# An expert tile built from the first two token tiles, a sixth weight buffer, and stores moved within the queue

## The chip, the core and the metric

The kernel runs on one core of a Trainium2 chip. The metric is the time of one execution on the device in microseconds (us); smaller is better. Engines are TensorE (PE in the rows, with PEld for its weight loads), VectorE (DVE), ScalarE (ACT), GpSimd (POOL) and SyncE (SP). A "q" behind an engine is its queue of DMA issues.

## The reference

One layer of an encoder over 512 tokens of width 1024, all float32: RMSNorm, one input projection, latent attention (8 heads, dense) and 2-D neighbourhood attention (8 heads), output projection added to x, and a mixture of experts:

```
p_g = softmax(h @ w_rg + b_rg)            # 4 groups, the best one is taken
le  = logits of the 4 experts of that group; top 2, softmax weights
a, u = h @ w_gate[e], h @ w_up[e]         # 1024 -> 256, for the token's 2 experts
x = x + sum over them of weight * (silu(a) * u) @ w_down[e]
```

There are 16 experts. Each has 2.1 MB of gate and up weights and 1.05 MB of down weights.

## The kernel before

Tokens are handled in T = 4 tiles of 128. After attention of a token tile, its sum x + attention (in `x_sb`) is normed, a router product gives logits, VectorE picks groups and experts (`logits_out`), TensorE computes each row's rank within its expert by products with a triangle of ones (`ranks`), VectorE turns ranks into row numbers (`ranks_out`), and GpSimd sends the tile's rows, with their weights and token numbers, to these places of a DRAM buffer `slot_rows` (`dispatch`, two sends a token tile, one for each of a token's two experts). That buffer was zeroed at the start.

Each expert has CAP = 96 places. They are read back as ITEMS = 12 expert tiles of 128 rows; tile g holds blocks of 32 rows (BLK), block b belonging to expert (4g + b) // 3. What overflows an expert goes to further tiles: number 12 always runs, up to EXTRA - 1 more run only when needed (`passes`). So tile 0 needs rows of all four token tiles.

For each expert tile g: its rows are loaded (`load_x`, on ScalarE's queue, all behind `s_disp`, the landing of all eight sends), TensorE turns them (`x_turns`), VectorE copies them out with the gain (`x_read`), `gate_up` multiplies (8 steps, 4 blocks), ScalarE does `silu`, VectorE the product (`hidden`), TensorE turns it (`hid_turns`), VectorE copies it (`hidden_read`), `down` multiplies, ScalarE and VectorE scale the two halves with the row's weight (`left_y`, `right_y`), and GpSimd adds the rows to the output in DRAM (`add`). TensorE's order is written out: gate_up(g), down(g-1), x_turns(g+2), hid_turns(g).

Expert weights pass through RING = 5 buffers each, filled in SP's queue, in order: buffer n % RING is asked for again when the last tile using its old expert is through gate_up (`s_gu`) or down (`s_dn`). Experts 0 to 4 are loaded during attention. SP's order at the end of attention is: load_gu(3), load_dn(3) and (4), load_gu(2), load_dn(2), load_gu(4), then the four stores of the sums to the output.

Every engine works through its own list in order; a wait holds all that is behind it.

Of the kernel before, what the change touches and what calls it, by code (L numbers as in the profile page):

```python
# [6 lines left out]
P = 128  # L7
# [39 lines left out]
EXTRA = TOP * SEQ // (CAP + 1)  # L47
FAR = 1 << 20
RING = 5
# [6 lines left out]
NK = K_MINE + ITEMS  # L56
# [7 lines left out]
def build(nc, x, x_turned, cols_d, rows_d, rope_d, rpb_d, consts_d, w_in_lat, w_in_k, w_in_q, w_in_v, w_qb, w_kvb, w_out, w_r,  # L64
# [8 lines left out]
    with ctx:  # L73
# [55 lines left out]
        junk = at(151, D_MODEL)  # L129
# [7 lines left out]
        sil = [at(140, F), at(141, F)]  # L137
        hid = [at(142, F), at(143, F)]
        hidT = [at(144, 2, P), at(145, 2, P)]
        y_sb = [at(110, D_MODEL), at(114, D_MODEL), at(136, D_MODEL)]  # L140
# [3 lines left out]
        x_hit = at(152, EXTRA, E)  # L144
        tag_sb = at(153, TILES, 2)
        tag_row = at(153.25, TILES, 1).bitcast(i32)
        x_prod = at(151, T, TOP, E)
# [35 lines left out]
        counts = sm(E)  # L183
        nmax = sm(2, H)
# [14 lines left out]
        GU = [bank[2], bank[3]]  # L199
# [35 lines left out]
        s_disp, s_over = sem("rows_dispatched"), sem("overflow_dispatched")  # L235
# [6 lines left out]
        s_add = [sem(f"y{r}_added_to_out") for r in range(3)]  # L242
# [20 lines left out]
        order += [("ms", 1, T - 1), ("h2", T - 1, 0), ("h2", T - 1, 1)]  # L263
        turn = {key: n for n, key in enumerate(order)}
        BY_ACT = ("k", "q", "nak", "naq")
# [44 lines left out]

        def turn_x(g, b):
            return 2 * g + b if g < 2 else 3 * g - 2 + b if g <= LAST else 3 * g + b

        def turn_h(g):
            return 3 * g + 6 if g < LAST - 1 else 2 * LAST + g + 2 if g <= LAST else 3 * g + 2

        def loads_of(g):

            return [(4 * g + b) // 3 if g < ITEMS else E + g - ITEMS for b in range(4)]

        def last_item(n):
            return (CAP * n + CAP - 1) // P if n < E else ITEMS + n - E

        def added_before(g):

            return 16 * (g // 3)
# [29 lines left out]
        def _(sp):  # L356
# [64 lines left out]

            sp.wait_ge(s_y, group["a", T - 1, 1] + 1)
            load_gu(3, 3)

# [15 lines left out]
            for g in range(LAST):  # L440
                for n in range(RING, E + 1):
# [3 lines left out]
                for n in range(RING, E + 1):  # L445
                    if last_item(n - RING) == g - 1:
                        sp.wait_ge(s_dn, 2 * g)
                        load_dn(n, expert(n))
# [13 lines left out]
            for g in range(LAST - 2, LAST + 1):  # L462
                sp.wait_ge(s_add[g % 3], added_before(g) + 16)

        @block.gpsimd
        def _(pool):
# [105 lines left out]
            def dispatch(t):  # L572
                pool.wait_ge(s_zero, 16)
                pool.wait_ge(s_h2s, t + 1)
                pool.wait_ge(s_wts, t + 1)
                pool.wait_ge(s_slot, t + 1)
                for k in range(TOP):
                    send(t, k, slots[0], ITEMS, s_disp)
# [23 lines left out]
            def add(g):  # L602
# [5 lines left out]
                    in_=y_sb[g % 3], in_offset=None,  # L608
                    bounds_check=SEQ - 1, oob_is_err=False, compute_op=ALU.add).then_inc(s_add[g % 3], 16)

            def added(g):

                pool.wait_ge(s_add[g % 3], added_before(g) + 16)
# [22 lines left out]
        def _(act):  # L636
# [77 lines left out]
            def x1_squares(t):  # L714
                act.wait_ge(s_x1, group["b", t, 1] + 1)
                link(nc.scalar.activation(junk, x_sb[:, t, :], ACT.Square, scale=D_MODEL ** -0.5,
# [101 lines left out]
            h2_rows(T - 1)  # L818
            top_exps(T - 1)
            nc.scalar.activation(junk[:, 0:1], junk[:, 0:1], ACT.Silu)  # L820

            def load_x(g):
                if g >= 3:
                    act.wait_ge(s_tt, turn_x(g - 3, 1) + 1)
# [3 lines left out]
            act.wait_ge(s_disp, 16 * TOP * T)  # L828
            for g in range(3):
                load_x(g)  # L830
            load_x(3)
# [7 lines left out]
            def left_y(g):  # L839
                act.wait_ge(s_dn, 2 * g + 1)  # L840
                act.wait_ge(s_tag, g + 1)
                if g >= 3:
                    act.wait_ge(s_add[g % 3], added_before(g))
                nc.scalar.activation(y_sb[g % 3][:, 0:512], YR[g % 2][0][:, :], ACT.Copy,
                                     scale=tag_sb[:, g, 0:1]).then_inc(s_ya, 1)

            for g in range(LAST + 1):
                if g == LAST:
                    left_y(g - 1)
                silu(g)  # L850
                if g + 4 <= LAST:
# [14 lines left out]
        def _(dve):  # L866
# [298 lines left out]
            def extras_out():  # L1165

                dve.wait_ge(s_counted, 1)
                nc.vector.tensor_copy(counts, bank[3][:, 0:E]).then_inc(s_countr, 1)
# [59 lines left out]
            def right_y(g):  # L1228
                dve.wait_ge(s_dn, 2 * g + 2)
                if g >= 3:  # L1230
                    dve.wait_ge(s_add[g % 3], added_before(g))
                nc.vector.tensor_scalar(y_sb[g % 3][:, 512:1024], YR[g % 2][1][:, :], tag_sb[:, g, 0:1], None,  # L1232
# [14 lines left out]
            x_read(0)  # L1247
            tile_tags(0)
            x_read(1)
            tile_tags(1)  # L1250
            extras_out()
            for g in range(LAST + 1):
# [3 lines left out]
                if 0 < g < LAST:  # L1256
# [5 lines left out]
                if g == 0:  # L1262
                    slots_out()
# [11 lines left out]
        def _(pe):  # L1275
# [150 lines left out]
            def side_turn(key):  # L1426
# [19 lines left out]
                if kind == "h2":  # L1446
                    pe.wait_ge(s_x1, group["b", t, b] + 1)
                    transposes(key, four(x_sb[:, t, :], b))

# [46 lines left out]
            def ranks(t):  # L1496
# [3 lines left out]
                for i in range(t + 1):  # L1500
                    last = nc.tensor.matmul(KB_OF[t][:, 32:32 + E], konst[:, K_ONE:K_ONE + P] if i < t else konst[:, K_TRI:K_TRI + P],
                                            sels[:, i, 0:E], start=(i == 0), stop=(i == t))
                last.then_inc(s_rank, 1)
# [75 lines left out]
            for i in range(T - 1):  # L1579
                nc.tensor.matmul(KB_OF[T - 1][:, 32:32 + E], konst[:, K_ONE:K_ONE + P], sels[:, i, 0:E],  # L1580
                                 start=(i == 0), stop=False)
            router(T - 1, (0,))
# [5 lines left out]
            for t in range(T):  # L1588
                last = nc.tensor.matmul(bank[3][:, 0:E], konst[:, K_ONE:K_ONE + P], sels[:, t, 0:E],
                                        start=(t == 0), stop=(t == T - 1))  # L1590
            last.then_inc(s_counted, 1)
            for p in (len(order) - 2, len(order) - 1):
                pe.wait_ge(*bank_read(p))

            def x_turns(g):
# [3 lines left out]
                for b in range(2):  # L1599
                    if g >= 2:  # L1600
                        pe.wait_ge(s_te, turn_x(g - 1 if g > 2 else 0, b) + 1)
# [5 lines left out]
            def gate_up(g, steps=range(KD)):  # L1607
                if 0 in steps:
                    pe.wait_ge(s_te, turn_x(g, 1) + 1)
                    if g == 0:  # L1610
                        pe.wait_ge(s_cnt, T)
                    if g == 1:
                        pe.wait_ge(s_countr, 1)
# [17 lines left out]
            def down(g):  # L1631
                pe.wait_ge(s_te, turn_h(g) + 1)
                if g >= 2:
# [13 lines left out]
            x_turns(0)  # L1647
            x_turns(1)
            for g in range(LAST + 1):
# [91 lines left out]
```

## Time and profile before

| | us |
|---|---|
| median of 3 runs | 507.0 (506.62 to 509.67) |
| the profiled execution's own time | 506.83 |
| its span, first to last instruction | 505.1 |
| TensorE busy in the span | 461.6 |
| mean granted TensorE clock | 0.968 of full |

The span is what the rows' times count in; 1.7 us of the execution's time lie around it. TensorE's clock has two levels, 2.4 GHz (granted 1.00) and 1.2 GHz (0.50).

### The profile page before, as it was taken

Reading aid. Unit: us, or ns where it says so; the run is one execution under the profiler, and the core shown is the slowest. Engines: PE = TensorE matmul, PEld = TensorE weight load, DVE = VectorE, ACT = ScalarE, POOL = GpSimd, SP = SyncE. Lnnn points to the kernel's source line nnn. Section 1 sums busy time; section 2 is a strip of 40 time slices with the busy share of each in tenths; the row PEclk is TensorE's granted clock in tenths of the full one; section 3 lists DMA queues with packets and bytes.
Section 4 is the critical chain, followed back from the end, with each engine's and each line's share of the span. In section 5 each row is a group of like instructions: output and inputs, shape, how many; then the busy total and the mean of one; then the engine's idle time right before and its main releaser. Section 6 shows DMA issues by size and latency. Waiting matters only on the chain.

```text
span 505.1 us, 7636 instructions
## 1 busy us (share of the span) xinstructions
PE 461.6 (91%) x2816; PEld 226.3 (45%) x2816; DVE 220.1 (44%) x688; ACT 145.8 (29%) x332; POOL 153.1 (30%) x163
## 2 busy tenths in 40 slices
PE   5999999989999999999999989519999999999982
PEld 3544545444555565555456556523333333333320
DVE  2144755525765545355566757607322222222210
ACT  1322504225455566444342533300000010110000
POOL 1151288877399910000000212200063111111121
PEclk9999999989999999999999999659999999999998
DMA  8999950006100000193000449973999999999731
GB/s 319 387 405 370 403 201 1 1 0 224 46 2 0 1 1 1 31 414 139 0 3 1 131 157 384 380 299 102 351 297 380 385 375 387 388 374 404 258 57 26
DMA packets 28745, 102.12 MB, mean 202 GB/s; under 512 B 3744, under 2 KB 5280, under 8 KB 28320
## 3 DMA queue, kind: packets, MB, share of 16 engines
q1 hardware_dynamic: 22080, 86.12, 44.0%
q0 software_dynamic: 4176, 8.42, 7.0%
q10 hardware_dynamic: 2448, 7.04, 3.8%
q8 instruction: 25, 0.41, 0.3%
q14 instruction: 16, 0.13, 0.1%
HBM read 79.48 MB, written 28.91 MB: 215 GB/s over the span
## 4 chain that ended last, share of the span: by engine, by line
PE 69%; DMA 8%; DVE 7%; POOL 7%; issue 4%; SPq 2%; ACT 1%; POOLq 0%; DVEq 0%
PE bank L1620 14%; PE bank L1298 14%; PE bank L1465 10%; PE bank L1641 6%; PE bank L1282 6%; DMA arena<-in_w_gu 6%; PE bank L1387 5%; PE bank L1370 5%; POOL small L477 3%; PE bank L1604 2%; SPq L393 2%; PE bank L1491 2%; PE bank L1411 2%; PE bank L1475 1%; DMA slot_rows<-arena,small 1%
## 5 line engine op out<-in xcount | busy, mean ns | idle before, releaser
L1298 PE MATMUL bank<-arena 128*128 128x512 f32 (+1 forms) x256 | 111.3, 585 | 5.6 <-DMA arena<-in_w_in_lat 5.6
L1620 PE MATMUL bank<-arena 128*32 128x512 f32 x832 | 92.6, 596 | 0.9 <-DMA arena<-in_w_gu 0.9
L1298 PEld LDWEIGHTS bank<-arena 128*128 128x128 f32 x256 | 48.3, 195 | 53.9 <-issue 53.9
L606 POOL DMA_INDIRECT out<-arena x13 | 20.2, 1551 | 138.7 <-DVE arena L1232 100.2
L1282 PEld LDWEIGHTS bank<-arena 128*128 128x128 f32 (+1 forms) x348 | 41.5, 139 | 37.5 <-issue 31.9
L1465 PE MATMUL bank<-arena 128*128 128x512 f32 x112 | 54.1, 605 | 0.5 <-issue 0.5
L1282 PE MATMUL bank<-arena 128*128 128x128 f32 (+1 forms) x348 | 49.8, 275 | 4.5 <-DVE arena L954 2.8
L1620 PEld LDWEIGHTS bank<-arena 128*32 128x32 f32 x832 | 26.1, 110 | 57.9 <-issue 56.8
L1641 PE MATMUL bank<-arena 128*32 128x512 f32 x416 | 47.1, 592 | 0.5 <-DVE arena L1225 0.5
L963 DVE COPY arena<-bank 128x512 f32<-128x512 f32 (+2 forms) x64 | 35.8, 581 | 20.9 <-PE bank L1282 20.9
L837 ACT ACTIVATE arena<-bank 128x256 f32<-128x256 f32 x13 | 5.0, 384 | 131.5 <-PE bank L1620 131.5
L481 POOL TENSOR_SCALAR small<-small 128x1 f32<-128x1 f32 x16 | 3.6, 224 | 121.9 <-DVE small L1002 72.2
L1218 DVE TENSOR_TENSOR arena<-arena,bank 128x256 f32<-128x256 f32 x13 | 5.5, 421 | 71.0 <-ACT arena L837 71.0
L696 ACT ACTIVATE arena<-arena,small 128x512 f32<-128x512 f32 (+2 forms) x64 | 34.7, 590 | 3.7 <-DVE small L971 3.6
L1082 DVE TENSOR_REDUCE small<-bank 128x1 f32<-128x512 f32 x32 | 22.1, 692 | 30.1 <-PE bank L1370 29.9
L477 POOL TENSOR_TENSOR small<-small 128x24 f32<-128x24 f32 (+2 forms) x7 | 29.8, 4263 | 16.3 <-DVE small L942 9.3
L1370 PE MATMUL bank<-arena 96*128 96x512 f32 x64 | 34.0, 616 | 0.0
L758 ACT ACTIVATE arena<-bank,small 128x512 f32<-128x512 f32 x32 | 22.0, 687 | 34.6 <-DVE small L1082 34.5
L1387 PE MATMUL bank<-arena 128*64 128x128 f32 x416 | 29.8, 280 | 1.6 <-DVE arena L963 1.6
L1387 PEld LDWEIGHTS bank<-arena 128*64 128x64 f32 x416 | 22.1, 136 | 16.2 <-issue 14.6
L497 POOL TENSOR_TENSOR arena<-arena 128x512 f32<-128x512 f32 (+2 forms) x20 | 22.1, 1122 | 22.7 <-issue 13.8
L1641 PEld LDWEIGHTS bank<-arena 128*32 128x32 f32 x416 | 13.6, 110 | 31.1 <-issue 30.3
(163 smaller groups left out, 506.3 us busy)
## 6 DMA issues: line engine op xcount, KB each, us to landing
arena<-in_w_gu SPq DMA_DIRECT2D x17, 2048.0 KB, 20.2
arena<-in_w_dn SPq DMA_DIRECT2D x17, 1024.0 KB, 20.5
slot_rows<-arena SPq DMA_DIRECT2D x1, 11308.0 KB, 46.4
arena<-slot_rows ACTq DMA_DIRECT2D x13, 514.0 KB, 6.8
arena<-in_w_out SPq DMA_DIRECT2D x2, 2048.0 KB, 8.3
arena<-in_x_turned SPq DMA_DIRECT2D x4, 512.0 KB, 7.8
arena<-in_x SPq DMA_DIRECT2D x4, 512.0 KB, 13.2
arena<-in_w_in_k SPq DMA_DIRECT2D x1, 2048.0 KB, 14.7
```

Source lines behind the costliest of these rows:

```text
L477: nc.gpsimd.tensor_tensor(v, v, mhalf[:, 0:n], ALU.pow).then_inc(s_root, 1)
L497: nc.gpsimd.tensor_tensor(dst, src, src, ALU.mult).then_inc(s_sqr, 1)
L696: nc.scalar.activation(probs, probs, ACT.Copy, scale=rsum[:, t % 2, u // MU, h:h + 1]).then_inc(s_ps, 1)
L963: nc.vector.tensor_copy(PT[u % 2][:, 0:blocks, :], TPB[p % 2][:, 0:blocks * P].rearrange("p (a b) -> p a b", a=blocks))\
L1082: nc.vector.tensor_reduce(nmax[:, u % 2, u % H:u % H + 1], SB[u % 2][:, :], AX.X, ALU.max, negate=True).then_inc(s_mx, 1)
L1282: last = nc.tensor.transpose(TPB[p % 2][0:s.shape[-1], b * P:(b + 1) * P], s, ident)
L1298: last = nc.tensor.matmul(product_bank(i)[:, 0:width], hT[:, t, k, :], w[:, k, :], start=(k == 0), stop=(k == KD - 1))
L1370: nc.tensor.matmul(SB[u % 2][:, :], qT[:, h, t * P:(t + 1) * P], kT[:, h, :], start=True, stop=True).then_inc(s_S, 1)
L1387: last = nc.tensor.matmul(OB[t % 2][DV * j:DV * (j + 1), pair * P:(pair + 1) * P], v[:, first + b, h * DV:(h + 1) * DV], PT[j][:, b, :], s ...
L1465: last = nc.tensor.matmul(YB[b][:, :], src[:, k, :], w_o[half][:, k, b * 512:(b + 1) * 512], start=(k == 0), stop=(k == 3))
L1620: last = nc.tensor.matmul(GU[g % 2][BLK * b:BLK * (b + 1), :], xT[g % 2][:, k, BLK * b:BLK * (b + 1)], w_gu[n % RING][:, k, :], start=(k = ...
L1641: last = nc.tensor.matmul(YR[g % 2][half][BLK * b:BLK * (b + 1), :], hidT[g % 2][:, k, BLK * b:BLK * (b + 1)], w_dn[n % RING][:, k, half * ...
```

## The change

Tile 0 is made of the first four experts' first 32 rows. Only token tiles 0 and 1 fill it: where an early expert has fewer than 32 rows in them, `pads` adds the missing number to its rank from token tile 2 on, so that no later row comes into tile 0. The remaining 64 places of these experts are tiles 1 and 2. Row load, turn and copy of tile 0 go before the last rank product; the copy is ScalarE's. gate_up(0) is split, with the counts inside, and down(0) is done at once. Tiles 0 to 2 are loaded by SP's queue, 1 and 2 behind the sixth w_gu load. That buffer lies over `x_sb`, so it waits for the stores. Stores 0 to 2 are moved ahead, one add buffer is given up, and two halves of `s_disp` count token tiles 0, 1 and 2, 3.

```diff
-EXTRA = TOP * SEQ // (CAP + 1)
+EARLY = P // BLK
+EXTRA = EARLY + (TOP * SEQ - EARLY * (CAP - BLK + 1)) // (CAP + 1)
-RING = 5
+RING = 6
-        w_gu = [at(kb, KD, 2 * F) for kb in (16, 48, 120, 32, 64)]
-        w_dn = [at(kb, 2, D_MODEL) for kb in (80, 171, 195, 179, 187)]
+        w_gu = [at(kb, KD, 2 * F) for kb in (16, 48, 120, 32, 64, 0)]
+        w_dn = [at(kb, 2, D_MODEL) for kb in (80, 171, 195, 179, 187, 136)]
-        y_sb = [at(110, D_MODEL), at(114, D_MODEL), at(136, D_MODEL)]
+        y_sb = [at(110, D_MODEL), at(114, D_MODEL)]
...
         def loads_of(g):
+            if g < 3:
+                return ([0, 1, 2, 3], [0, 0, 1, 1], [2, 2, 3, 3])[g]
             return [(4 * g + b) // 3 if g < ITEMS else E + g - ITEMS for b in range(4)]
...
# SP
+            store(0)
+            store(1)
             sp.wait_ge(s_y, group["a", T - 1, 1] + 1)
             load_gu(3, 3)
+            store(2)
...
             load_dn(2, 2)
+            sp.wait_ge(s_disp[0], 16 * TOP * 2)
+            sp.dma_start(xg[0], x_dram[0:P, :]).then_inc(s_xg[0], 16)
             sp.wait_ge(s_y, len(groups))
             load_gu(4, 4)
-            for t in range(T):
-                sp.wait_ge(s_x1, group["b", t, 1] + 1)
-                sp.dma_start(out[t], x_sb[:, t, :]).then_inc(s_out, 16)
+            store(T - 1)
+            sp.wait_ge(s_out, 16 * T)
+            sp.wait_ge(s_h2s, T)
+            sp.wait_ge(s_tp, turn["h2", T - 1, 1] + 1)
+            load_gu(5, 5)
+            sp.wait_ge(s_disp[1], 16 * TOP * 2)
+            for g in range(1, 3):
+                sp.dma_start(xg[g], x_dram[g * P:(g + 1) * P, :]).then_inc(s_xg[g], 16)
+            load_dn(5, 5)
# ScalarE
             h2_rows(T - 1)
+            for b in range(2):
+                p = turn["early", 0, b]
+                act.wait_ge(s_tp, p + 1)
+                for k in range(4 * b, 4 * b + 4):
+                    last = nc.scalar.activation(xT[0][:, k, :], TPB[p % 2][:, (k - 4 * b) * P:(k - 4 * b + 1) * P], ACT.Copy,
+                                                scale=cols[:, C_FFN + k:C_FFN + k + 1])
+                last.then_inc(s_tpa[p % 2], 1)
             top_exps(T - 1)
...
# VectorE, ranks_out(t)
+                if t == 1:
+                    link(nc.vector.tensor_tensor(pads, konst[:, K_FLOOR:K_FLOOR + E], KB_OF[t][:, 64:64 + E], ALU.subtract))
+                    nc.vector.tensor_scalar(pads, pads, 0.0, None, ALU.max).then_inc(s_pad, 1)
+                nc.vector.scalar_tensor_tensor(early, KB_OF[t][:, 32:32 + E], BLK - 0.5, konst[:, K_LOW:K_LOW + E],
+                                               ALU.is_lt, ALU.mult)
...
-                link(nc.vector.tensor_tensor(early, slot, over, ALU.add))
+                link(nc.vector.tensor_tensor(early, early, slot, ALU.add))
+                link(nc.vector.tensor_tensor(early, early, over, ALU.add))
# TensorE
             router(T - 1, (1,))
+            for b in range(2):
+                side_turn(("early", 0, b))
+
             pe.wait_ge(s_sel, T)
...
+            def counted():
+                pe.wait_ge(s_cnt, T - 1)
+                for t in range(T):
+                    nc.tensor.matmul(bank[4][:, 0:E], konst[:, K_ONE:K_ONE + P], sels[:, t, 0:E], start=(t == 0), stop=False)
+                nc.tensor.matmul(bank[4][:, 0:E], ident, pads, start=False, stop=True).then_inc(s_counted, 1)
...
             def down(g):
                 pe.wait_ge(s_te, turn_h(g) + 1)
+                if g == 0:
+                    pe.wait_ge(s_cnt, T)
+                    pe.wait_ge(s_countr, 1)
...
-            x_turns(0)
+            gate_up(0, range(2))
+            counted()
+            gate_up(0, range(2, KD))
+            hid_turns(0)
+            down(0)
             x_turns(1)
-            for g in range(LAST + 1):
+            x_turns(2)
+            for g in range(1, LAST + 1):
                 gate_up(g, range(2 if g == LAST else KD))
-                if g > 0:
+                if g > 1:
                     down(g - 1)
```

## Rows read from the trace of the kernel before

**Rows 1.** Page: busy tenths in 40 slices of 12.6 us, and the adds' group

```profile
PE   5999999989999999999999989519999999999982
...
PEclk9999999989999999999999999659999999999998
DMA  8999950006100000193000449973999999999731
...
L606 POOL DMA_INDIRECT out<-arena x13 | 20.2, 1551 | 138.7 <-DVE arena L1232 100.2
```

**Rows 2.** Chain that ended last, 328 to 464: start, length, what was waited for

```profile
328.76 6.20 DMA slot_rows<-arena,small
334.98 3.32 DMA arena<-slot_rows
...
350.99 7.00 PE bank L1620 x64
357.99 3.43 PE bank L1641 x32
361.42 1.02 PE bank L1604 x8
362.45 0.22 PE bank L1628 x2
...
428.56 28.33 DMA arena<-in_w_gu
...
457.03 7.07 PE bank L1620 x64
```

**Rows 3.** Timeline of PE: start, length, line, what, [idle before and its releaser]

```profile
319.69 1.90 PE L1491 MATMUL bank<-arena 128*128 128x20 f32 x8 [0.78 <-DVE arena L883]
324.89 0.61 PE L1586 MATMUL bank<-arena 128*128 128x16 f32 x2 [3.31 <-DVE arena L1041]
...
338.44 3.64 PE L1604 MATMUL bank<-arena 128*128 128x128 f32 x16 [11.24 <-DMA arena<-slot_rows]
...
491.94 3.64 PE L1641 MATMUL bank<-arena 128*32 128x512 f32 x32 [0.52 <-DVE arena L1225]
```

**Rows 4.** Windows: length, busy time of PE, PEld, DVE, ACT, POOL, then PEclk, DMA share, GB/s

```profile
280.00:284.00 4.00, 4.00 (x17) 2.21 (x18) 3.47 (x22) 2.21 (x8) 1.05 (x1) 1.00 0.00 0
...
321.60:338.44 16.84, 2.32 (x11) 2.24 (x11) 4.37 (x31) 2.06 (x5) 3.97 (x4) 0.50 0.87 347
338.44:342.08 3.64, 3.64 (x20) 3.31 (x24) 2.33 (x7) 0.00 (x0) 0.00 (x0) 0.50 0.57 198
...
349.65:456.89 107.24, 106.44 (x964) 37.73 (x963) 32.29 (x95) 10.04 (x19) 20.59 (x17) 1.00 1.00 362
...
369.73:456.89 87.16, 86.36 (x784) 30.48 (x776) 24.71 (x68) 8.58 (x16) 19.00 (x16) 1.00 1.03 373
349.65:351.20 1.55, 1.55 (x14) 1.07 (x17) 1.13 (x3) 0.39 (x1) 0.00 (x0) 1.00 0.44 40
```

**Rows 5.** Timelines of ACT and DVE, single instructions of the kinds added or moved

```profile
312.81 0.28 ACT L711 ACTIVATE arena<-bank 128x128 f32<-128x128 f32 x1 [5.91 <-PE bank L1387]
...
323.96 0.30 ACT L727 ACTIVATE arena<-arena 128x4 f32<-128x4 f32 x1 [4.22 <-DVE arena L1037]
...
325.82 0.18 DVE L1053 TENSOR_TENSOR arena<-arena 128x16 f32<-128x16 f32 x1
```

**Rows 6.** DMA issues of four windows, by start (310.1, 323.6, 312.8, 318.0): median us to landing

```profile
slot_rows<-arena,small POOLq DMA_INDIRECT x1, 6.2
...
slot_rows<-arena,small POOLq DMA_INDIRECT x1, 8.8
...
arena<-in_w_dn SPq DMA_DIRECT2D x1, 1024.0 KB, 7.7
...
out<-arena SPq DMA_DIRECT2D x1, 512.0 KB, 15.7
```

**Rows 7.** Timeline of POOL: the second send of token tile 1

```profile
310.13 0.97 POOL L566 DMA_INDIRECT slot_rows<-arena,small  x1 [0.30 <-issue]
```

More of the change, by code:

```diff
@@ L420, in _, with store @@
             load_dn(1, 1)
+            def store(t):
+                sp.wait_ge(s_x1, group["b", t, 1] + 1)
+                sp.dma_start(out[t], x_sb[:, t, :]).then_inc(s_out, 16)
+            store(0)
+            store(1)
             sp.wait_ge(s_y, group["a", T - 1, 1] + 1)
             load_gu(3, 3)
+            store(2)
             sp.wait_ge(s_S, 2 * MU)
@@ L1245, in tile_tags @@
                 nc.vector.tensor_tensor(tag_sb[:, g, 0:1], tag_sb[:, g, 0:1], tag_sb[:, g, 1:2], ALU.add).then_inc(s_tag, 1)
-            x_read(0)
             tile_tags(0)
-            x_read(1)
-            tile_tags(1)
+            dve.wait_ge(s_counted, 1)
+            nc.vector.tensor_copy(counts, bank[4][:, 0:E]).then_inc(s_countr, 1)
             extras_out()
-            for g in range(LAST + 1):
+            hidden(0)
+            hidden_read(0)
+            slots_out()
+            right_y(0)
+            for g in range(1, 3):
+                x_read(g)
+                tile_tags(g)
+            for g in range(1, LAST + 1):
                 if g == LAST:
@@ L1448, in side_turn @@
                     transposes(key, four(x_sb[:, t, :], b))
+                if kind == "early":
+                    pe.wait_ge(s_xg[0], 16)
+                    transposes(key, four(xg[0], b))
             def out_projection(key, part):
@@ L1500, in ranks @@
                 for i in range(t + 1):
+                    if i == t == 2:
+                        pe.wait_ge(s_pad, 1)
+                        nc.tensor.matmul(KB_OF[t][:, 32:32 + E], ident, pads, start=False, stop=False)
                     last = nc.tensor.matmul(KB_OF[t][:, 32:32 + E], konst[:, K_ONE:K_ONE + P] if i < t else konst[:, K_TRI:K_TRI + P],
                                             sels[:, i, 0:E], start=(i == 0), stop=(i == t))
+                if t == 1:
+                    for i in range(2):
+                        last = nc.tensor.matmul(KB_OF[t][:, 64:64 + E], konst[:, K_ONE:K_ONE + P], sels[:, i, 0:E],
+                                                start=(i == 0), stop=(i == 1))
                 last.then_inc(s_rank, 1)
@@ L1608, in gate_up @@
                 if 0 in steps:
-                    pe.wait_ge(s_te, turn_x(g, 1) + 1)
                     if g == 0:
-                        pe.wait_ge(s_cnt, T)
+                        for b in range(2):
+                            pe.wait_ge(*bank_read(turn["early", 0, b]))
+                        pe.wait_ge(s_mx, 2 * MU)
+                    else:
+                        pe.wait_ge(s_te, turn_x(g, 1) + 1)
                     if g == 1:
-                        pe.wait_ge(s_countr, 1)
+                        pe.wait_ge(s_lgr, T)
                     if g >= 2:
@@ L1709 @@
     p = np.arange(P, dtype=f32)
+    mine = (P * p[:ITEMS] + p[:, None]) // CAP
+    mine[:, 0] = p // BLK
+    for g in (1, 2):
+        mine[:, g] = 2 * (g - 1) + p // (2 * BLK)
     konst = np.concatenate([
         np.triu(np.ones((P, P), f32), 1), np.ones((P, P), f32), np.tile(p[:E], (P, 1)),
-        np.tile(CAP * p[:E], (P, 1)), np.tile(p[:EXTRA], (P, 1)), np.tile(p[:E] % G, (P, 1)), p[:, None] + P * p[:T] - FAR,
-        np.full((P, 1), FAR), (P * p[:ITEMS] + p[:, None]) // CAP], axis=1).astype(f32)
+        np.tile(np.where(p[:E] < EARLY, P - BLK + 2 * BLK * p[:E], CAP * p[:E]), (P, 1)), np.tile(p[:EXTRA], (P, 1)), np.tile(p[:E] % G, (P, 1)), p[:, None] + P * p[:T] - FAR,
+        np.full((P, 1), FAR), mine, np.tile(np.where(p[:E] < EARLY, BLK - P - BLK * p[:E], 0), (P, 1)),
+        np.tile(np.where(p[:E] < EARLY, BLK, 0), (P, 1))], axis=1).astype(f32)
     def by_expert(v, blocks):
```

112 lines of the change are left out of this document (58 added, 54 removed).

## The prediction, made before the changed kernel was run

> **What bounds the kernel now.** I first read the page, to see where TensorE is not busy, then the chain of waits through that place, then the engines' timelines and the DMA issues around it. The page shows TensorE at nine tenths almost everywhere, with one hole around slices 25 to 27, where its granted clock also falls, and DMA at nine tenths or more in every slice from 28 to 36 [rows 1]. The hole is the hand-over from attention to experts. The chain shows what it consists of: after the last router product TensorE has only two small products (ranks and counts) to do, the last token tile's rows are sent (6.20 us from the last send to landing), tile 0's rows are read back (3.32 us), and only then do the transposes of tiles 0 and 1 start, at 338.44 [rows 2, 3]. Of the 16.84 us from 321.60 to 338.44 TensorE is busy 2.32 [rows 4].
>
> From there the expert tiles run at one pace: gate/up 7.00, down 3.43, next rows turned 1.02, hidden turned 0.22, in all 11.67 us a tile (350.99 to 362.66) [rows 2]. Once, ahead of tile 10, TensorE waits for a weight transfer that was asked for 28.33 us earlier; the wait itself is short (457.03 instead of 456.09, where the pace would have put it) [rows 2]. But the DMA share is 1.03 over the 87 us before [rows 4]. So there are two limits close together: TensorE, and the weights' stream. A change that only lets TensorE start earlier would run into the second. I count in starts of gate/up: S1 is tile 1's (350.99 before), S10 tile 10's (457.03 before); behind S10 nothing of the change acts.
>
> **What the change is worth, part by part.** The sum is made against the profiled execution, 506.83 us with a span of 505.1; the median of the runs is 507.0, so I carry the difference over to it unchanged.
>
> *Is the work the same?* The page shows 13 adds to the output, so 12 fixed tiles and one for overflow [rows 1]. I counted the reference's routing on the given inputs: the four early experts get 46, 64, 53 and 69 rows, padding adds 2, 6, 3 and 0, all under 96, and only one expert (165 rows) overflows, by 69. It stays at 13 tiles, so gate/up and down cost the same.
>
> *Rows of tile 0.* They now need only the first two token tiles. The second of tile 1's sends started at 310.13 [rows 7]. Ahead of it the change puts two padding operations and two on the early ranks on VectorE, about 0.2 each [rows 5], and two products (four records) on TensorE, and a store of 0.5 MB goes before it: 1.2 us, so 311.3. Landing took 6.2 in a calm stretch and 8.8 in a full one [rows 6]; I take 6.2 plus 0.5 for the store, as the transfers ahead are otherwise those of before: 318.0. The load of tile 0's rows then stands behind one w_dn load, asked for at 312.80 and landed after 7.7, at 320.5 [rows 6]. Free, it takes 3.3 [rows 2]. So the rows are in between 321.3 and 324; I take 323.0.
>
> *TensorE waits for them.* Router products ended at 321.6 [rows 3]; eight more small records (four, two and two) at 0.12 to 0.24 each, some inside waits, put that at 322.3. So TensorE idles 0.7, turns tile 0 in 1.8 at the low clock (half of the 3.64 that two tiles took [rows 3]), to 324.8. Queued behind this wait is the last rank product, which could have started at 324.89 + 0.5 anyway: no loss as long as the rows land by about 323.5.
>
> *ScalarE, and who waits behind it.* It now copies eight blocks of 128x128, 0.28 each with overlap of about 0.05 [rows 5], the last four after the second half is turned: to about 326.0. The exponentials of the last token tile started at 323.96 [rows 5]; they now come at 326.0, VectorE's weights wait for them, and two more VectorE operations follow: the last dispatch moves by 2.1 us, its second send from 328.76 to 330.9. Landing after 6.2 to 8.8 [rows 6]: 337.1 to 339.7, I take 338. That was the head of the critical chain before, and is 3 us later now; what pays is that TensorE has work meanwhile.
>
> *What fills the hole.* Gate/up of tile 0 from 326.1: 7.07 at full clock, and up to 2 us more because the granted clock in that stretch was 0.50 (1.2 GHz) from 321.6 to 342.1, until 3.6 us after TensorE took up continuous work again at 338.44 [rows 4]. With continuous work from 323 I take 2 us as lost, as much as before. Inside it the counts, ten small records, 1.5. Then silu, product, turn and copy stand open (1.87 at the last tile, where the down product starts at 491.94, of which 0.52 shows as idle ahead of the last down product [rows 3]), then down 3.6. Together 326.1 + 9.1 + 1.5 + 1.9 + 3.6 = 342.2. The extras' arithmetic on VectorE, some 3.9 us, lies beside gate/up, and the new wait of down(0) for ranks and counts (both done by 335) costs nothing; without that cover it would delay down(0) by up to 3.9.
>
> *Rows of tiles 1 and 2* now go through the weights' queue. Asked for at 338, free they land at 341.3, but the sixth w_gu load (2 MB) stands before them. It waits for all four stores. The last store now follows the fifth w_gu load; it took 15.7 us when asked for in the same place [rows 6], hence 331 to 333, so the sixth load is asked for there and shares the engines with the last dispatch: 3.1 MB at 373 GB/s [rows 4] is 8.4 us, to 340. Tile 1's rows: 342.5, tile 2's 1.3 later. The turns and reads end at 345.0. That is S1, 6.0 earlier than before; bounds 343.5 (free transfers) and 348 (both at the slow end).
>
> *What tile 1 no longer finds before it.* Between S1 and S2 the down product of tile 0 (3.43) is done already: S2 = S1 + 7.07 + 1.02 + 0.35 = S1 + 8.4, and S10 = S1 + 8.4 + 8 x 11.67 = 446.8 if weights never lack: 10.2 earlier than 457.03.
>
> *The weights' stream.* The sixth buffer lets one expert (3.1 MB) load in the calm stretch before 350. But the next loads (experts 6 and 7) are asked for only when gate/up of tile 1 ends, S1 + 7.1 = 352.1, hardly later than the 349.65 at which the stream began before. From 349.65 to 456.89 the core moved 107.24 us x 362 GB/s = 38.8 MB [rows 4]. Of this fall away expert 5 (3.1 MB, less the 1.05 of one w_dn that now stands ahead of the decisive load), one tile's rows (0.5) and one add (0.5): 35.7 MB. At 373 GB/s that is 95.7 us; without the wasted start (only 40 GB/s in its first 1.5 us) and the four overflow sends that now fall before 352 perhaps 93. With 1.5 us of start, expert 14 lands at 446.6 to 449.3; I take 448.3, as 373 is the rate of the like stretch. That is later than 446.8, so the stream decides: **8.7 us gained**, 1.5 of the possible 10.2 given back.
>
> The same stretch against a rule: the row gives 373 GB/s with the share at 1.03. The Trainium skill ("DMA: Bandwidth & Descriptors", section Specifications) gives about 358 GB/s as the limit from HBM for one core. The trace is already above that, so I keep the row; by 358 the 35.7 MB would take 99.7 us and the gain would be near 4 us.
>
> *Edits at nothing.* The stores of sums 0 to 2 move to where the DMA idles (share 0.00 at 280 to 284 [rows 4]) and SP has nothing to ask; their cover is that SP waits for the attention steps there anyway; otherwise a w_dn load would come up to 1.3 us late, with over 20 us of slack. Two instead of three output buffers: an add is asked for 1.1 us after its tile and lands within 13, the buffer is wanted again after 23.3. One tile more to zero is 0.5 MB in the first 80 us, waited for only by the first send, long after.
>
> **The rivals.**
> *A: TensorE alone decides.* The stream is faster than 373 because it begins more evenly; S10 = 446.8 or a little less: gain 10 to 11.5, 495.5 to 497. For it: the overflow sends, which have small packets, leave the full stretch in part. Against: the share is at 1.03 already [rows 4].
> *B: late rows and a dry stream.* Nothing is asked of the weights' queue before tile 1's gate/up ends, so each microsecond of S1 goes through to the end. And the rows of tiles 1 and 2, moved from ScalarE's queue to SP's, stand behind up to 2.1 MB of weights instead of sharing the engines with it: at 373 GB/s [rows 4] 5.6 us on top of the 3.32 [rows 2], S1 up to 348, and with 96 us of stream the gain is 3.5 to 6: 501 to 503.5. (A rule speaks for this: the Trainium skill, "DMA: Bandwidth & Descriptors", section Queues, rings and completion order, has each queue's descriptors taken in order on an engine and the queues served in turn. No row here has a row load behind a weight load in one queue.)
> *C: nothing comes of it* (the low clock lasts through tile 0, ScalarE's copies and the ranks pass the delay on in full): tile 0 then ends hardly before the next rows, S1 near 350, gain 0 to 3: 504 to 507.
> *D: slower.* TensorE's in-order wait for tile 0's rows holds the last rank product, and with it the last dispatch, tiles 1 and 2 and the stream. Its price is one to one beyond 323.5. It decides once the rows land 8.7 later, after 332, 14 us after being asked for. The stores took 15.7 so [rows 6], but behind 2 MB of weights; tile 0's rows stand before that load. At 15.7 the result would be about 509.
>
> **How the numbers follow.** Forecast (stream decides, gain 7 to 10) 0.52; A 0.12; B 0.21; C 0.10; D 0.05. The likeliest gives 507.0 - 8.7 = 498.3 us. The low end takes in most of A (495.8), the high end most of B (502.8); C and D stay out. One per cent, about what a measurement can tell here, is 5.1 us, so faster by more than that takes the forecast, A and two thirds of B, 0.79; within it the rest of B and C, 0.16; slower 0.05.
>
> **What the profile after would show.** Right: gate/up records of tile 0 from about 326, with the counts between; no TensorE gap over 2 us from 322 to 345 except before tile 1; tile 1's gate/up at 343.5 to 348; one or two short waits for in_w_gu ahead of tiles 9 or 10, which start near 436 and 448; DMA share about 1 from 353 to 466. The forecast is wrong if tile 0's rows land after 325, if the first wait for weights comes before tile 8 or never, or if tile 1 starts outside those bounds.

## The result and the profile after

The changed kernel takes 503.89 us in the median (502.5 to 505.57, 7 runs) against 507.72 us before on the same chips: ratio 0.9932, 95% interval 0.9915 to 0.9950. By the ratio it is 3.5 us faster, where 8.7 were forecast, and the median lies outside the range (495.8 to 502.8). The profiled execution took 502.5 us, with a span of 500.6.

The page of the changed kernel, busy tenths in 40 slices of 12.5 us and the group of the adds, which answer to [rows 1]:

```profile
PE   5999999989999999999999998896999999998982
...
PEclk9999999999999999999999989879999999999997
DMA  8999960005100000094010349799599999999531
...
L638 POOL DMA_INDIRECT out<-arena x13 | 20.2, 1550 | 130.6 <-DVE arena L1276 101.4
```

Tiles are still 13. The hole around slice 26 (counted from 0) is filled; slice 27 is left at six tenths, and most of the missing time is there. The chain of the changed kernel through the hand-over (start, length, what was waited for), to set against [rows 2]:

```profile
311.54 9.40 DMA slot_rows<-arena,small
320.96 3.30 DMA arena<-slot_rows
...
332.43 5.44 DMA slot_rows<-arena,small
...
338.27 9.45 DMA arena<-slot_rows
...
348.86 7.00 PE bank L1685 x64
...
357.26 7.00 PE bank L1685 x64
```

The chain goes through two row loads. Tile 0's takes 3.30 us, as before. The one of tiles 1 and 2 takes 9.45, and ahead of it, in SP's queue, stands the sixth w_gu load. SP's timeline:

```profile
320.96 0.34 SPq L460 DMA_DIRECT2D arena<-slot_rows  x1
321.35 0.43 SPq L406 DMA_DIRECT2D arena<-in_w_gu  x1
321.82 0.50 SPq L441 DMA_DIRECT2D out<-arena  x1
334.96 0.37 SPq L406 DMA_DIRECT2D arena<-in_w_gu  x1
337.88 0.82 SPq L470 DMA_DIRECT2D arena<-slot_rows  x2
```

The sixth load waits for the last store, which landed 13 us after it was asked for. So the load went out at 334.96, and the rows' loads 2.9 us behind it. It took 10.2 us to land, to 345.1, while tile 1's rows waited. TensorE's timeline shows what that costs:

```profile
324.31 1.97 PE L1330 MATMUL bank<-arena 128*128 128x128 f32 x8 [1.28 <-DMA arena<-slot_rows]
...
327.74 3.64 PE L1685 MATMUL bank<-arena 128*32 128x512 f32 x16 [0.93 <-issue]
...
339.81 3.64 PE L1709 MATMUL bank<-arena 128*32 128x512 f32 x32 [0.52 <-DVE arena L1269]
346.49 1.09 PE L1666 MATMUL bank<-arena 128*128 128x128 f32 x8 [3.04 <-DMA arena<-slot_rows]
347.76 1.09 PE L1666 MATMUL bank<-arena 128*128 128x128 f32 x8 [0.19 <-DMA arena<-slot_rows]
348.79 7.07 PE L1685 MATMUL bank<-arena 128*32 128x512 f32 x64
...
452.57 7.07 PE L1685 MATMUL bank<-arena 128*32 128x512 f32 x64 [1.76 <-DVE arena L1269]
```

Tile 0 is through its down product at 343.45, tile 1's rows are there at 346.49, and its gate/up begins at 348.8. Tile 2's follows 8.4 us later, as forecast, and from there the pace is that of before, 11.67 a tile, up to tile 10, which starts at 452.57 instead of 457.03: the 4.5 us by which the span is shorter. The 1.76 us ahead of it are a wait for weights, although VectorE is named: VectorE's copy is not what gate/up needs there, a run with a lighter stream (e4) has no such wait, and e1's trace names the weights for the like one. The stream, in the window that answers to the 107 us of [rows 4]:

```profile
355.86:452.57 96.71, 94.90 (x860) 34.37 (x859) 27.97 (x80) 9.65 (x18) 21.54 (x17) 1.00 1.02 374
```

96.71 us at 374 GB/s are 36.2 MB.

### The profile page after: what moved, and what is told of

Read it like the earlier page. It is cut to its first block, busy times and chain, and to the rows that moved or that the text cites. A ratio compares the mean times of both kernels' runs of the same rounds, so it can differ in the third digit from the quotient of the medians.

```text
span 500.6 us, 7676 instructions
## 1 busy us (share of the span) xinstructions
PE 464.3 (93%) x2826; PEld 226.8 (45%) x2826; DVE 220.1 (44%) x696; ACT 147.8 (30%) x340; POOL 152.9 (31%) x163
## 4 chain that ended last, share of the span: by engine, by line
PE 72%; DVE 8%; POOL 7%; DMA 6%; issue 5%; ACT 1%; POOLq 0%; SPq 0%; DVEq 0%
PE bank L1685 17%; PE bank L1346 14%; PE bank L1516 10%; PE bank L1709 8%; PE bank L1330 6%; PE bank L1418 5%; PE bank L1435 5%; POOL small L509 3%; DMA slot_rows<-arena,small 3%; DMA arena<-slot_rows 3%; PE bank L1666 2%; PE bank L1459 2%; DVE arena L987 1%; POOL arena L365 1%; DVE arena L989 1%
## 5 line engine op out<-in xcount | busy, mean ns | idle before, releaser
L1685 PE MATMUL bank<-arena 128*32 128x512 f32 x832 | 94.1, 603 | 2.7 <-DVE arena L1269 1.8
L1346 PEld LDWEIGHTS bank<-arena 128*128 128x128 f32 x256 | 48.2, 195 | 53.5 <-issue 53.1
L1330 PEld LDWEIGHTS bank<-arena 128*128 128x128 f32 (+1 forms) x356 | 42.9, 141 | 39.3 <-issue 32.3
L1330 PE MATMUL bank<-arena 128*128 128x128 f32 (+1 forms) x356 | 51.4, 277 | 5.7 <-DVE arena L994 2.8
L1516 PE MATMUL bank<-arena 128*128 128x512 f32 x112 | 55.6, 620 | 0.6 <-issue 0.6
L1685 PEld LDWEIGHTS bank<-arena 128*32 128x32 f32 x832 | 26.7, 111 | 58.7 <-issue 56.7
L1709 PE MATMUL bank<-arena 128*32 128x512 f32 x416 | 47.1, 593 | 1.0 <-DVE arena L1269 1.0
L1516 PEld LDWEIGHTS bank<-arena 128*128 128x128 f32 x112 | 19.5, 194 | 18.7 <-issue 18.7
```

What stands on the lines that cost most here:

```text
L1330: last = nc.tensor.transpose(TPB[p % 2][0:s.shape[-1], b * P:(b + 1) * P], s, ident)
L1346: last = nc.tensor.matmul(product_bank(i)[:, 0:width], hT[:, t, k, :], w[:, k, :], start=(k == 0), stop=(k == KD - 1))
L1516: last = nc.tensor.matmul(YB[b][:, :], src[:, k, :], w_o[half][:, k, b * 512:(b + 1) * 512], start=(k == 0), stop=(k == 3))
L1685: last = nc.tensor.matmul(GU[g % 2][BLK * b:BLK * (b + 1), :], xT[g % 2][:, k, BLK * b:BLK * (b + 1)], w_gu[n % RING][:, k, :], start=(k = ...
L1709: last = nc.tensor.matmul(YR[g % 2][half][BLK * b:BLK * (b + 1), :], hidT[g % 2][:, k, BLK * b:BLK * (b + 1)], w_dn[n % RING][:, k, half * ...
```

## The experiments

Ratios are to the kernel before on the same chip; in brackets stand the 95% intervals. Three chips were used: one for e1 to e4, one for e5 to e8, one for e9 to e11. The changed kernel has 0.9932 in its first runs and 0.9891 in e11, which is 2.1 us apart. So a difference of about 2 us between ratios from different chips shows nothing by itself; where a reading rests on less, it rests on the traces.

Two theories run through the expectations. Q: tile 1's rows are late because 2 MB was asked for ahead of them in the same queue. V: the end is set by the volume of weights still to come, wherever the rows stand.

**e1: rows ahead of the sixth load.**

```diff
+            sp.wait_ge(s_disp[1], 16 * TOP * 2)
+            for g in range(1, 3):
+                sp.dma_start(xg[g], x_dram[g * P:(g + 1) * P, :]).then_inc(s_xg[g], 16)
             sp.wait_ge(s_out, 16 * T)
...
             load_gu(5, 5)
-            sp.wait_ge(s_disp[1], 16 * TOP * 2)
-            for g in range(1, 3):
-                sp.dma_start(xg[g], x_dram[g * P:(g + 1) * P, :]).then_inc(s_xg[g], 16)
             load_dn(5, 5)
```

> The changed kernel with the loads of tiles 1 and 2's rows asked for ahead of the sixth w_gu load instead of behind it. Theory Q (queue): in the changed kernel the rows landed 8 to 9.5 us after being asked for because 2 MB stood before them; free they take 3.3 and 4.6, so tile 1's turns start when down(0) is through (343.5 instead of 346.5), gate/up of tile 1 at 346 instead of 348.8, and as the weights' stream is asked for at its end, the whole end moves by 2.5 to 3 us: about 0.995 of the changed kernel. Rival V (volume): what ends the kernel is the amount of weights still to be loaded, and the sixth w_gu load now comes 3.5 us later, so tile 10 starts where it did (452.6) or up to 1 us later; TensorE only waits longer for weights.

Measured: 499.13 us, 0.9835 [0.9816, 0.9854]. That is 8.4 us faster than before, and 4.9 faster than the changed kernel by the two ratios (2.8 by the changed kernel's ratio in e11; the medians are 4.8 and 5.1 apart). Its SP and TensorE timelines and the stream's window:

```profile
336.90 0.81 SPq L466 DMA_DIRECT2D arena<-slot_rows  x2
337.83 0.38 SPq L406 DMA_DIRECT2D arena<-in_w_gu  x1
```

```profile
342.35 1.97 PE L1666 MATMUL bank<-arena 128*128 128x128 f32 x16
344.49 7.07 PE L1685 MATMUL bank<-arena 128*32 128x512 f32 x64 [0.17 <-DVE arena L1253]
...
447.92 7.07 PE L1685 MATMUL bank<-arena 128*32 128x512 f32 x64 [1.53 <-DMA arena<-in_w_gu]
```

```profile
351.56:447.79 96.23, 94.83 (x858) 33.71 (x858) 27.73 (x80) 9.65 (x18) 21.19 (x17) 1.00 1.02 375
```

TensorE finds the rows in when it wants them. Tile 1 starts 4.3 us earlier than in the changed kernel and tile 10 4.65: the stream is as long as it was (96.2 us) and only begins earlier. V falls, and what Q says of the order of asking holds. The gain was more than the 2.5 to 3 us expected; 1.1 us of it is that in this profile tile 0's part was earlier.

**e2: the same rows from ScalarE's queue, the sixth load left where it is.**

```diff
-            for g in range(1, 3):
-                sp.dma_start(xg[g], x_dram[g * P:(g + 1) * P, :]).then_inc(s_xg[g], 16)
...
                     act.wait_ge(s_disp[1], 16 * TOP * 2)
+                    load_x(1)
+                    load_x(2)
                     load_x(3)
```

> The changed kernel with the rows of tiles 1 and 2 loaded from ScalarE's queue (as before the change), at the same moment, the sixth w_gu load left where it is. Theory Q: the rows share the engines with the 2 MB instead of standing behind it and land after 5 to 7 us instead of 8.5 to 9.5: gate/up of tile 1 at 346 to 347, end 1.5 to 2.5 us earlier. If the DMA engines' bandwidth alone counted and not the order of a queue, they would land as late as in the changed kernel and the time would stay. Rival V: no change of the end in either case.

Measured: 505.64 us, 0.9949 [0.9928, 0.9970], no better than the changed kernel. TensorE's timeline, and two windows whose last three numbers are granted clock, DMA share and GB/s:

```profile
347.53 1.09 PE L1666 MATMUL bank<-arena 128*128 128x128 f32 x8 [3.51 <-DMA arena<-slot_rows]
349.73 1.97 PE L1666 MATMUL bank<-arena 128*128 128x128 f32 x8 [1.11 <-DMA arena<-slot_rows]
351.63 8.95 PE L1685 MATMUL bank<-arena 128*32 128x512 f32 x64
```

```profile
347.53:351.63 4.10, 2.99 (x16) 2.42 (x17) 2.47 (x7) 0.00 (x0) 0.00 (x0) 0.63 0.51 176
351.63:360.50 8.87, 8.87 (x65) 2.19 (x64) 1.18 (x5) 0.00 (x0) 0.00 (x0) 0.78 0.12 47
```

Tile 1's rows land 8.5 us after being asked for, no earlier than in SP's queue (8.6), where 5 to 7 were expected. So a queue of their own did not save them. With e1, the reading is that what counts is the 2 MB asked for just before, with which the rows share the engines. One thing differs besides: the sixth w_dn load (1 MB) no longer stands behind the rows in SP's queue but is asked for at the same moment, 338.98. A run with that load held back was not made, so the share of the queue alone is not shown. And something new shows: in the wait the granted clock falls, and gate/up of tile 1 takes 8.95 us instead of 7.07.

**e3: last store ahead of the fifth load**, so that the sixth can go out early.

```diff
+            store(T - 1)
             sp.wait_ge(s_y, len(groups))
             load_gu(4, 4)
-            store(T - 1)
```

> The changed kernel with the last store asked for ahead of the fifth w_gu load. The sixth load waits for that store's landing; it is then asked for near 326 instead of 335 and is through before the last rows are sent back. Theory Q: rows of tiles 1 and 2 find an empty queue, land 3.3 to 4.6 us after being asked for; but the last dispatch shares the engines with two w_gu loads and lands 1 to 3 us later. Net gain 0 to 3 us, gate/up of tile 1 at 346 to 349. Rival V: the sixth load is out of the way 9 us earlier but nothing else is asked for in that time, so the stream from tile 1 on is as long: no change.

Measured: 502.35 us, 0.9903 [0.9887, 0.9920]. The dispatch was hit as expected (8.27 us to landing instead of 5.44), the rows still took 6.7, tile 1's gate/up started at 347.9 and took 8.01 us, with the clock down again. A gain over the changed kernel is not shown (1.5 us by the first ratio, none by e11's); moving the load forward moves the collision to the dispatch.

**e4: a lighter stream**, w_dn loads from expert 6 on cut to 256 columns of one block, so that down products from there use old weights.

```diff
+                if n >= 6:
+                    sp.dma_start(w_dn[n % RING][:, 0, 0:256], row(w_dn_d, e)[:, 0, 0:256]).then_inc(s_wdn[n % RING], 16)
+                else:
...
```

> The changed kernel with the w_dn loads from expert 6 on cut to an eighth (the output is not the reference's): 0.13 instead of 1.05 MB each, so the stream from tile 1 on is 9 to 10 MB or a quarter shorter. If TensorE's pace from tile 1 on set the end and the stream only the 1.76 us ahead of tile 10, the end moves by 1.8 to 2 us (to 500.6 in time for 502.5) and no wait for weights is left. If the stream held the kernel more than the trace shows (slower matmuls through contention, late rows), the end moves by more than 3.

Measured: 501.97 us, 0.9891 [0.9874, 0.9908]; no wait for weights is left in its trace. The ratio is 2.1 us under the changed kernel's first one and equal to that of e11, so what the stream costs is read from traces: from S1 to S10 the changed kernel takes 103.8 us, and e7 below, without a wait for weights, 101.8. That is 2 us; the rest of what is missing lies before tile 1.

**e5: early tile and moved stores, but five weight buffers** (`RING = 5`, no load_gu(5, 5), no load_dn(5, 5)).

> The changed kernel with five weight buffers, so without the sixth w_gu and w_dn loads; early tile and moved stores stay. Theory Q: the rows of tiles 1 and 2 find a free queue and land within 5 us, tile 1's gate/up starts at 344.5 to 345.5, as in e1. Then the stream from tile 1's end on is 3.1 MB longer (39.3 MB at 374 GB/s, 105 us), weights for tile 10 land near 457 and the whole is as before the change (ratio 0.995 to 1.002), with waits for weights of 8 to 10 us in all. If the sixth buffer were worth nothing, the time would be that of e1 (0.984).

Measured: 509.87 us, 1.0045 [1.0015, 1.0074], slower than the 0.995 to 1.002 expected. TensorE's timeline, of the fastest of its five runs (506.87 us):

```profile
344.21 7.07 PE L1683 MATMUL bank<-arena 128*32 128x512 f32 x64 [0.17 <-DVE arena L1251]
...
408.25 9.00 PE L1683 MATMUL bank<-arena 128*32 128x512 f32 x64 [8.53 <-DMA arena<-in_w_gu]
```

Tile 1 starts at 344.2, the earliest of all. Then one wait of 8.53 us for weights, already ahead of tile 6 and not of tile 10, gives it all back, and gate/up behind it takes 9.00 instead of 7.07. Tile 10 starts at 456.9, as before the change. Time won at the hand-over is worth nothing here without the sixth buffer.

**e6: sixth buffer, layout, two add buffers and moved stores, but no early tile.** The edits are those lines of the change, on the kernel before; tiles 0 to 2 are read back on ScalarE's queue.

> The kernel before with the memory layout, the sixth weight buffers, two add buffers and the moved stores of the changed one, but without the early tile: rows of tiles 0 to 2 are read back on ScalarE's queue. Theory Q, as e2 left it (bytes asked for before the rows count, not the queue): the sixth w_gu load is asked for near 334, right before the rows at 335, the rows land after 8 us instead of 3.3, tile 0's turns begin near 343 and not at 338.4, nothing hides it, and the 0.9 us wait ahead of tile 10 goes: 3 to 4.5 us slower than before, ratio 1.006 to 1.009. If row loads were not held up by a weight load: 0.998.

Measured: 511.37 us, 1.0065 [1.0043, 1.0086]. The size was as expected, the place was not: the expectation had the row loads late, and it was the dispatch. Its chain:

```profile
328.64 10.21 DMA slot_rows<-arena,small
338.86 0.02 issue
338.88 3.30 DMA arena<-slot_rows
```

Without the early tile SP asks for the sixth w_gu and w_dn loads at 327.04 and 327.45, so they meet the last dispatch, which takes 10.21 us to land instead of 6.20 [rows 2]; the rows behind it are free again at 3.30. Each half of the change alone makes the kernel slower.

**e7: e1 with w_gu loads ahead of w_dn loads in each round of the stream**, the order of before.

```diff
             for g in range(LAST):
                 for n in range(RING, E + 1):
-                    if last_item(n - RING) == g - 1:
-                        sp.wait_ge(s_dn, 2 * g)
-                        load_dn(n, expert(n))
-                for n in range(RING, E + 1):
                     if last_item(n - RING) == g:
                         sp.wait_ge(s_gu, g + 1)
                         load_gu(n, expert(n))
+                for n in range(RING, E + 1):
+                    if last_item(n - RING) == g - 1:
+                        sp.wait_ge(s_dn, 2 * g)
+                        load_dn(n, expert(n))
```

> e1 (rows ahead of the sixth load) with the order of before in the stream loop, w_gu loads ahead of the w_dn loads in each round. In e1 TensorE still waits 1.5 us ahead of tile 10 for a w_gu load that lands 29.7 us after being asked for. With one w_dn load (1.05 MB, 2.8 us) less ahead of it the wait goes: 1.2 to 1.5 us faster than e1, ratio to before about 0.981. If the volume as such were short and not the order, the wait would come back ahead of tile 11 or 12, or ahead of a down product.

Measured: 497.11 us, 0.9774 [0.9755, 0.9792]. By the ratios 3.1 us faster than e1, more than the 1.5 expected, and no wait for weights from tile 1 on is in its trace. The wait removed is 1.5 us; the rest of the difference is not explained, and the two ran on different chips. Its profiled run (499.96 us) is the slowest of its six, and TensorE's timeline shows some of the reason:

```profile
331.30 1.89 PE L1654 MATMUL bank<-arena 128*128 128x16 f32 x8
...
333.54 7.10 PE L1685 MATMUL bank<-arena 128*32 128x512 f32 x48
```

The last 48 records of tile 0's gate/up take 7.10 us here and 5.36 in e1: the clock stayed at its low level until into them.

**e8: three extra products in the wait for tile 1's rows.**

```diff
             down(0)
+            for i in range(3):
+                nc.tensor.matmul(TPB[0][:, :], ident, w_dn[0][:, 0, 0:512], start=True, stop=True)
             x_turns(1)
```

> The changed kernel with three extra products of 128x512 (about 2.8 us, result unused) between tile 0's down product and the wait for tile 1's rows. In some runs of the changed kernel (505.5 us) and in the profiles of e2, e3 and e4 the granted clock falls in that wait and gate/up of tile 1 takes 8.0 to 8.95 us instead of 7.07. If that is what spreads the changed kernel's runs over 502.5 to 505.6, this one is never over 503.5, tile 1's gate/up is 7.07, and it is as fast as the fast runs, since the products lie in the wait. If the spread comes from elsewhere, it stays, and the extra work costs 0 to 2.8 us.

Measured: 501.74 us, 0.9880 [0.9861, 0.9899]; five of six runs at 501.4 to 502.0, one at 503.74, so "never over 503.5" is a miss by one run. The timeline:

```profile
341.68 2.84 PE L1721 MATMUL bank<-arena 128*128 128x512 f32 x6
345.53 1.09 PE L1666 MATMUL bank<-arena 128*128 128x128 f32 x8 [1.01 <-DMA arena<-slot_rows]
...
347.84 7.07 PE L1685 MATMUL bank<-arena 128*32 128x512 f32 x64
```

The added work cost nothing that shows, and tile 1's gate/up runs at 7.07. The mean granted clock was 0.980 or 0.981 in all six runs, and 0.971 to 0.982 in the 13 of the changed kernel.

**e9 and e10: two edits on e7.** e9 puts `top_exps(T - 1)` ahead of ScalarE's eight copies; e10 puts `store(2)` behind the load of tile 0's rows.

> e7 with ScalarE's exponentials of the last token tile ahead of its eight copies of tile 0, not behind them. In the changed kernel VectorE waits 1.98 us for them, and the last dispatch with it. Theory Q: the dispatch comes 2 us earlier, but in e7 the rows of tiles 1 and 2 are in before TensorE wants them, so nothing is gained, and gate/up of tile 0 starts 0.3 us later: within 0.5 us of e7. If the delayed dispatch were still on the path that sets the end, 1.5 to 2 us would be gained.

> e7 with the store of the third sum asked for behind the load of tile 0's rows, not ahead of the weight loads at 300. In the changed kernel the second send of token tile 1 took 9.4 us to land (6.2 before the change) and TensorE waits 1.28 us for tile 0's rows. If the moved store costs the 3 us, tile 0's rows come 1.3 us or more earlier, TensorE does not wait, and the end moves 1 us forward. If the landing is late because of the other loads in flight (w_gu, w_dn), as 0.5 MB is only 1.4 us at 374 GB/s, the gain is under 0.5 us.

Measured: e9 499.07 us, 0.9812 [0.9779, 0.9845]; e10 496.18 us, 0.9762 [0.9733, 0.9791]. e9 gains nothing, as expected: the last dispatch's second send goes out at 330.6 by its trace, 1.9 us earlier than in the changed kernel, but the rows were in time already. Whether it loses cannot be told, since its runs spread over 5 us. e10 cannot be told from e7 either. The send of token tile 1 landed after 5.2 us in it, but tile 0's rows were there only at 324.4, 7 us after being asked for (a w_dn load went out 2.7 us ahead of them in SP's queue), and TensorE still waited 0.89 us. And among the kernels with the third store early it the same landing took 9.4 in one profile and 6.1 in that of e11, so a single profile doesn't price the store. What makes that landing vary stays open.

**e11: the changed kernel once more.**

> The changed kernel once more, unaltered, for its own spread beside e9 and e10 on one chip. Theory Q with the clock: runs lie in two groups, near 502.5 where the granted clock holds through the wait for tile 1's rows and near 505.5 where it falls. If the two groups were only two chips, all runs here lie in one.

Measured: 504.23 us (500.75 to 504.79), 0.9891 [0.9866, 0.9916]. SP's timeline and the windows ahead of tile 1:

```profile
332.94 0.37 SPq L406 DMA_DIRECT2D arena<-in_w_gu  x1
340.57 0.82 SPq L470 DMA_DIRECT2D arena<-slot_rows  x2
```

```profile
343.50:348.18 4.68, 0.02 (x3) 0.00 (x1) 0.75 (x1) 0.00 (x0) 0.00 (x0) 1.00 0.99 365
348.18:351.50 3.32, 3.32 (x20) 2.92 (x24) 2.33 (x7) 0.00 (x0) 0.00 (x0) 0.56 0.40 160
```

In this profile (504.79 us) the wait is 4.66 us instead of 3.04, the clock falls behind it (0.56 over the next 3.3 us), and the two tiles' turns take 3.32 us instead of 2.2. Here the sixth load went out 2 us earlier than in the first profile, and the last dispatch landed 8.2 us after its send instead of 5.4, so the rows were asked for 2.7 us later. On one chip the runs lie at 500.75, 502.64 and four near 504.4: so the spread is not one of chips. Two sharp groups they are not.

## Why the prediction was wrong

The step that failed is the one headed "Rows of tiles 1 and 2". It had the sixth load asked for at 331 to 333, through at 340, tile 1's rows in at 342.5 and S1 at 345.0, with 348 as the slow end. In the trace the load went out at 335.0, the rows landed at 346.5 and 347.7, and S1 was 348.8. The mechanism was named (rival B); its size was put in the forecast at 1.2 us over a free landing, where it is 5. The forecast had the sixth load through 2 us after the rows were asked for. In the trace it landed 7 us after that: from 337.87 to 346.49 the core moved 8.6 us at 406 GB/s, 3.5 MB, before tile 1's rows were in.

Two things in the sum were off. The sixth load's request: SP now asks for the fifth w_gu load and the last store only behind tile 0's row load, which the forecast itself had at 318.0 or later, and 15.7 us from there is 334, not 331 to 333 (three stores fewer stand ahead, but the sum does not say what that saves). In the trace the row load went out at 320.96, because the send before it landed after 9.40 us (forecast 6.7), and the fifth load at 321.35. Before the change it went out at 315.54:

```profile
315.54 0.37 SPq L389 DMA_DIRECT2D arena<-in_w_gu  x1
```

That move was priced nowhere. And the bytes: the 3.1 MB left out the rows of tile 3 (0.5 MB), which ScalarE asks for at 338.04. That the request's time alone does not settle it is shown by e11: there the load went out at 332.9, within the forecast, yet the last dispatch landed at 340.6, the rows at 348.2, and S1 was 351.4. In four profiles of this hand-over (the changed kernel, e11, and e4 and e8, which ask for the same loads up to there) tile 1's rows landed 7.6 to 8.6 us after being asked for. The forecast had 4.5.

e1 takes this term out and gives 8.4 us, S1 at 344.5 and tile 10 at 447.9, against 8.7, 345.0 and 448.3 in the forecast. So the rest of the sum held, within the 1.3 to 1.6 us by which tile 0's part was late in the changed kernel's trace. That the totals agree so well is partly luck: the forecast's 345.0 holds 1.2 us of collision, and e1's 344.5 holds none but a later tile 0. Of the signs of being wrong that the prediction named, one came true: tile 1 started at 348.8, outside 343.5 to 348.

Point by point, in the changed kernel's trace:

| step | forecast | measured |
|---|---|---|
| landing of the second send of token tile 1 | 6.7 us, at 318.0 | 9.4 us, at 320.9 |
| tile 0's rows in | 323.0 | 324.3 |
| TensorE's wait for them | 0.7 | 1.28 |
| gate/up of tile 0 starts | 326.1 | 327.7 |
| last send / its landing | 330.9 / 338 | 332.4 / 337.9 |
| down of tile 0 through | 342.2 | 343.5 |
| sixth w_gu load asked for | 331 to 333 | 335.0 |
| sixth w_gu load through | 340 | 345.1 |
| tile 1's rows in | 342.5 | 346.5 |
| S1 | 345.0 | 348.8 |
| volume and time of the stream | 35.7 MB, 95 to 97 us | 36.2 MB, 96.7 us |
| wait ahead of tile 10 | 1.5 | 1.8 |

*The clock* was the second omission. The forecast priced the low clock in the hole, but not that a wait of some 3 us ahead of tile 1 may bring it back. Where it did (e2, e3, e4, e11), turns and gate/up of tile 1 took 1 to 3 us longer. The first profile shows the wait without the fall. The clock explains only in part why other runs are slower than the profiled one: one with a mean clock of 0.978 also reached 505.6. How much of the gap between 502.5 and 505.6 is clock and how much later rows was not separated.

*The rule on queues.* I used the Trainium skill ("DMA: Bandwidth & Descriptors", section Queues, rings and completion order) to argue that rows in ScalarE's queue would share instead of standing behind. Whether they share no run here shows by itself. e2 shows that it didn't help: with the engines full, the rows landed 8.5 and 10.3 us after being asked for. The limit of 358 GB/s that the Trainium skill gives ("DMA: Bandwidth & Descriptors", section Specifications) did not hold the stream: it ran at 374 and 375 GB/s over 96 us (changed kernel and e1), so the row was the right thing to reckon with.

*The rivals.* B happened, and somewhat beyond its own bounds (S1 348.8 against 348, median 503.9 against 503.5). A did not; V, which I held against Q afterwards, fell with e1, but e5 shows that the stream decides at once when one buffer fewer is there. D's mechanism is real and was small here: 1.28 us of wait for tile 0's rows, which were in 0.8 us after the 323.5 from which D counts. Counting tiles from the routing was right: 13.

The experiments led to a version that beats both: e7, 0.9774 [0.9755, 0.9792], about 11.5 us under the kernel before, and e10, which cannot be told from it.

## What to carry to other kernels

When a freed buffer lets a big prefetch go out, look at what small transfer on the critical path is asked for in the next few microseconds: order the small one first; a queue of its own did not save it here (e2). Two changes that look separable may need each other: here an earlier start of TensorE and an earlier start of the weights' stream were each a loss alone and a gain together. And a landing time is to be worked out from when everything ahead of it is asked for, with those times carried at their late end, too.

## What the runs showed of the hardware

Waits of TensorE of similar length ahead of tile 1's turns did different things to the granted clock. One of 3.04 us left it at full level (changed kernel). After one of 3.40 us (e4), one of 4.66 (e11), one of 3.51 followed by one of 1.11 (e2), and one of only 2.77 followed by one of 0.65 (e3) it fell: 0.75 over the next 3.0 us in e4, 0.79 over 3.5 in e3, 0.56 over 3.3 in e11, 0.63 over 4.1 and then 0.78 over 8.9 us in e2. By these windows the low level (1.2 GHz) held for some 3 us in e11 and 7 in e2, an estimate. What decides between the two outcomes these runs do not show. With 2.84 us of useless products and 1.01 us of idle time in the wait (e8) the clock stayed up, and the kernel was no slower for them.

A 2 MB and a 1 MB load, asked for 1.6 and 1.2 us ahead of a dispatch's last send, went with a landing of 10.2 us for that send instead of 6.2 (e6 against the kernel before). A 0.5 MB row load that took 3.3 us with no weight load beside it (the kernel before, e6) took 7.6 to 8.6 us when a 2 MB load had been asked for 3 to 8 us ahead of it.
